# mLSTM projections: the gate panels' high parts made by GpSimd, and the low-rank blocks turned inside the gates' projection

## The reference, cut to what matters

```python
proj = h @ w_in                                    # [512, 1024] @ [1024, 1992]
u, v_m, o_pre, i_pre, f_pre, c_q, c_kv, k_r = split(proj)   # 512, 512, 512, 4, 4, 256, 128, 64 columns
u_c = silu(causal_dwconv(u, conv_w, conv_b))
q_m, k_m = u_h @ wq_m, u_h @ wk_m                  # per head
ig, fg = i_pre + b_igate, f_pre + b_fgate          # the recurrence's gates
hm = rmsnorm(mlstm_chunkwise(q_m, k_m, v_m, ig, fg))
y_m = sigmoid(o_pre) * hm                          # o_pre: the "gate panels" of the change
q_a = rmsnorm(c_q) @ w_uq                          # 256 -> 768, low rank
kv = rmsnorm(c_kv) @ w_ukv                         # 128 -> 1024, low rank
... per-head rmsnorm, rope, causal attention, rmsnorm -> y_a
out = concat([y_m, y_a]) @ w_out
```

## Time and profile before

| what | before |
|---|---|
| median of 3 runs | 1885.59 us (1885.58, 1885.59, 1886.93) |
| the profiled execution's own time | 1886.09 us |
| its span, first to last instruction | 1884.3 us |
| TensorE (PE) busy | 1847.6 us, 98% |
| GpSimd (POOL) busy | 1364.4 us, 72% |
| VectorE (DVE) busy | 907.7 us, 48% |
| ScalarE (ACT) busy | 756.6 us, 40% |

### The profile page before, as it was taken

One profiled execution on the slowest core, in us unless ns is written; L12 is line 12 of the kernel. 1 busy time (PEld: TensorE's weight loads), 2 busy tenths in 40 slices (PEclk: granted clock), 3 DMA queues, 4 the chain that ended last, 5 costly groups with the idle time before them and its releaser, 6 DMA issues.

```text
span 1884.3 us, 26203 instructions
## 1 busy us (share of the span) xinstructions
PE 1847.6 (98%) x9597; PEld 1560.9 (83%) x9597; DVE 907.7 (48%) x1797; ACT 756.6 (40%) x1459; POOL 1364.4 (72%) x1211
## 2 busy tenths in 40 slices
PE   7999999999999999999999999999999999999999
PEld 6888888888878887888888888987679888888887
DVE  6677777762028875355403412726753455203410
ACT  4577777754027763242102201567643522001100
POOL 8766666698854559879888988663524579888885
PEclk9999999999999999999999999999999999999999
DMA  7322222223432232422432333221122223332342
GB/s 223 110 68 68 68 68 67 68 68 90 111 105 75 63 95 90 136 68 89 112 89 90 104 96 89 70 82 45 46 68 90 90 67 90 94 107 90 89 110 69
DMA packets 213613, 165.71 MB, mean 88 GB/s; under 512 B 14478, under 2 KB 209873, under 8 KB 213122
## 3 DMA queue, kind: packets, MB, share of 16 engines
q1 hardware_dynamic: 208134, 149.32, 27.0%
q10 hardware_dynamic: 5372, 14.98, 2.4%
HBM read 161.11 MB, written 7.37 MB: 89 GB/s over the span
## 4 chain that ended last, share of the span: by engine, by line
PE 55%; POOL 5%; issue 2%; ACT 2%; DVE 2%; DMA 0%; POOLq 0%; ACTq 0%; DVEq 0%; SPq 0%
PE bank L401 42%; PE bank L483 4%; POOL w_lo L3254 3%; PE bank L427 1%; POOL w_hi L3246 1%; PE bank L1588 1%; PE bank L1612 1%; PE bank L3004 1%; PE bank L1810 1%; PE bank L1789 1%; PE bank L646 1%; PE bank L1799 0%; PE bank L2652 0%; PE bank L1598 0%; POOL x_features L750 0%
## 5 line engine op out<-in xcount | busy, mean ns | idle before, releaser
L3254 POOL TENSOR_TENSOR w_lo<-w_raw,w_hi 128x512 fp32r<-128x512 f32 (+1 forms) x572 | 718.0, 1288 | 207.6 <-ACT w_hi L1435 198.2
L3246 POOL TENSOR_TENSOR w_hi<-w_raw,one 128x512 fp32r<-128x512 f32 (+1 forms) x428 | 441.2, 1062 | 223.2 <-PE bank L401 199.6
L401 PE MATMUL bank<-h_hi,w_hi 128*128 128x512 f32 x952 | 377.4, 396 | 1.1 <-POOL w_lo L3254 0.8
L401 PE MATMUL bank<-h_hi,w_lo 128*128 128x512 f32 x952 | 371.9, 391 | 0.0
L401 PE MATMUL bank<-h_lo,w_hi 128*128 128x512 f32 x952 | 371.1, 390 | 0.0
L401 PE MATMUL bank<-a_hi,w_hi 128*128 128x512 f32 x832 | 326.0, 392 | 1.7 <-POOL w_lo L3254 1.4
L401 PE MATMUL bank<-a_hi,w_lo 128*128 128x512 f32 x832 | 324.0, 389 | 0.0
L401 PE MATMUL bank<-a_lo,w_hi 128*128 128x512 f32 x832 | 323.8, 389 | 0.0
L401 PEld LDWEIGHTS bank<-h_hi,w_lo 128*128 128x128 f32 x952 | 178.7, 188 | 39.0
L401 PEld LDWEIGHTS bank<-h_hi,w_hi 128*128 128x128 f32 x952 | 178.9, 188 | 35.5 <-issue 1.4
L401 PEld LDWEIGHTS bank<-h_lo,w_hi 128*128 128x128 f32 x952 | 179.1, 188 | 33.4
(11 more groups left out here) (506 smaller groups left out, 3021.6 us busy)
## 6 DMA issues: line engine op xcount, KB each, us to landing
w_raw<-in_w_ff SPq DMA_DIRECT2D x32, 1024.0 KB, 5.5
w_raw<-in_w_in SPq DMA_DIRECT2D x31, 1024.0 KB, 5.4
w_raw<-in_w_mlp_in SPq DMA_DIRECT2D x16, 1024.0 KB, 5.3
w_raw<-in_w_mlp_out SPq DMA_DIRECT2D x16, 1024.0 KB, 5.6
w_raw<-in_w_in SPq DMA_DIRECT2D x26, 512.0 KB, 4.2
w_raw<-in_w_ssd_out SPq DMA_DIRECT2D x8, 1024.0 KB, 5.6
bias_rows<-bias_row ACTq DMA_DIRECT2D x1, 4096.0 KB, 15.6
w_raw<-in_w_attn_out SPq DMA_DIRECT2D x4, 1024.0 KB, 5.8
```

What stands on the lines that cost most here:

```text
L401: mm = pe.matmul(bank[:, 0:ntok], a, b[:, koff + k, 0:ntok], start=(k == 0 and n == 0), stop=(k == L.kb - 1 and n == 2))
L3246: pool.tensor_tensor(w_hi[:, slot, part], raw[:, slot, part], one[:].broadcast_to([P, n]), ALU.mult).then_inc(split_hi, 1)
L3254: ins = pool.tensor_tensor(w_lo[:, slot, part], raw[:, slot, part], w_hi[:, slot, part].bitcast(F32), ALU.subtract)
```

## The change

Two edits. The gate panels leave `HIGH_BY_ACT`, and ScalarE's two calls of `split_high_act` for them go; GpSimd thereby makes their high parts with the instructions of line 3246, ahead of their low parts. And TensorE does the first two of L_if's 8 contraction steps, then the wait for `lt["low"]` and the 12 transposes of CQT and CKT, then L_if's other six steps; ScalarE's copy of the gates moves behind its three copies of the turned blocks.

```diff
-        HIGH_BY_ACT = ... + [L.p0 for L in (L_va, L_low, L_vb, *L_gate_m)] + ...
+        HIGH_BY_ACT = ... + [L.p0 for L in (L_va, L_low, L_vb)] + ...
...
             pe_panel_tokens(pe, L_vb, 0, 0, h_x)
-            pe_panel(pe, L_if, 0, 0, h_x)
+            pe_panel(pe, L_if, 0, 0, h_x, ks=range(0, 2))
             pe.wait_ge(lt["low"], 1)
             low = tp_n["pe"]
             pe_to_features(pe, CQT, T, 2, banks[4:6])
             pe_to_features(pe, CKT, T, 1, banks[6:7])
+            pe_panel(pe, L_if, 0, 0, h_x, ks=range(2, DB))
             pe.wait_ge(lt["kr"], 1)
...
             tokens_act(act, L_vb, 0, lambda t: VM[:, t, 3:5, 0:128], only=1)
-            gates_in_act(act)
             act_to_features(act, a_x, 8, 2, lambda b: colv("cq", b), T, banks[4:6])
             act_to_features(act, a_x, 10, 1, lambda b: colv("ckv"), T, banks[6:7])
+            gates_in_act(act)
             act.wait_ge(lt["kr"], 2)
             act.activation(KR, banks[7][:], ACT.Copy)
-            split_high_act(act, L_gate_m[0])
             for i in range(2 * T):
                 q_block_act(act, i)
...
             tokens_act(act, L_gate_m[0], 0, lambda t: OM[:, t, 0:256], ACT.Sigmoid)
-            split_high_act(act, L_gate_m[1])
             for i in range(2 * T):
                 k_block_act(act, i)
```

More of the change, by code:

```diff
@@ L1416, in ssd_stage_pe @@
             pe_panel(pe, L_ssd_out, 0, 0, a_x, ks=range(0, 2 * GROUPS - 2))
-        HIGH_BY_ACT = list(range(L_ssd[1][0].p0, L_gate_ssd.p0)) + [L_attn[1][0].p0, L_attn[1][1].p0] + [L_mlp[0][0][0].p0 + 1, L_u.p0 + 1] + [L.p0 for L in (L_va, L_low, L_vb, *L_gate_m)] + [L_out2.p0 + 2, L_out2.p0 + 3] + list(range(L_kx.p0, L_vx.p0 + 2))
+        HIGH_BY_ACT = list(range(L_ssd[1][0].p0, L_gate_ssd.p0)) + [L_attn[1][0].p0, L_attn[1][1].p0] + [L_mlp[0][0][0].p0 + 1, L_u.p0 + 1] + [L.p0 for L in (L_va, L_low, L_vb)] + [L_out2.p0 + 2, L_out2.p0 + 3] + list(range(L_kx.p0, L_vx.p0 + 2))
         high_by_act, low_by_dve = sem("high_by_act"), sem("low_by_dve")
```

## The result

The changed kernel takes 1889.08 us (median of 18 runs, 1887.4 to 1892.1), the kernel before 1885.79 us (median of 18 runs beside them, 1884.8 to 1887.4): a ratio of 1.0017 with a 95% interval of 1.0011 to 1.0024. That is 3.3 us slower, just inside 0.2%, outside my range, and to the side that I had given to rival (C) alone. The profiled execution took 1887.78 us, with a span of 1886.1.

The account below looks back on a forecast made before the run. TensorE, busy 98% of the span, bounds the kernel, with 5.5 us of waits between 1257 and 1300 us. Gains 0.8 (turn) and 1.8 (panels), less 0.6, 0.1 and 0.1, make 1.8 us: median 1883.8 us, range 1881.9 to 1886.4.

Parts of the forecast that it names:

- rival (C): Second gate panel late if GpSimd's two halves take over 12.1 us; slower, 1886.0 to 1886.8 us; chance 8%.
- Part 1: Turn of CQT and CKT moved inside the gates' projection: gain 0.8 us, at least 0.7, at most 0.95.
- (a): First gate panel's low part on GpSimd slows VectorE's softplus: cost 0.6 us taken, from nothing to 1.3.
- (b): VectorE's gate rows beside GpSimd's second gate panel: cost 0.1 us taken, ends -0.6 and +0.7.
- Rival B: The lock: softplus waits out the low part, first scan pays 0.7; gain only 0.6 us, 1884.6 to 1885.4; chance 18%.
- The first gate panel costs nothing: Panel ready on GpSimd at 1266.7, TensorE asks at 1269.3: cover 2.6 us, worst case 0.4 lost; work queued behind costs nothing.

Follow-up runs that it names:

- first_yield: Changed kernel with the second gate panel's high part back on ScalarE and GpSimd pausing for VectorE twice in the first panel's low part; ratio 0.9997.
- hold: Changed kernel, but GpSimd waits for VectorE's fourth query normalization before beginning the second gate panel; 1888.39 against 1886.11 us, ratio 1.0010.
- fill: Changed kernel with 14 extra matmuls of 128x512 ahead of the fourth turn, in TensorE's wait before the fifth; 1888.18 us, ratio 1.0003.
- turn_only: Changed kernel with both gate panels' high parts back on ScalarE, leaving only the turn inside the gates' projection; 1886.70 against 1886.93 us, ratio 1.0000.
- high_only: Changed kernel with the gates' projection in one piece again, both gate panels' high parts still on GpSimd; 1888.36 against 1886.93 us, ratio 1.0007.
- fill_turns: Changed kernel with 28 extra transposes ahead of the fourth turn as filler for TensorE's wait; one execution, 1890.52 us.
- first_panel: Changed kernel with the second gate panel's high part back on ScalarE, only the first's on GpSimd; 1888.57 us, ratio 1.0009.
- small_pieces: Changed kernel, but GpSimd splits the second gate panel in 16 pieces of 128x128 per part instead of 4 of 128x512; 1889.76 us, ratio 1.0016.
- half_yield: hold_yield, but ScalarE makes half of the second gate panel's high part and GpSimd the other half; 1885.52 against 1887.22 us, ratio 0.9991.
- hold_yield: Changed kernel with the pauses of first_yield and GpSimd's wait of hold, both gate panels on GpSimd; 1888.05 against 1887.22 us, ratio 1.0005.
- second_panel: Changed kernel with the first gate panel's high part back on ScalarE, only the second's on GpSimd; 1887.00 us, ratio 1.0001.

## Why the prediction was wrong

**Part 1 was right in its place.** I took 0.8 us for the turn. L_uq starts 1.04 us earlier in every kernel that has it, and the gate columns, not the low parts, are what is late next. Without the overlaps in its way, 0.7 us of it reach the fifth turn (first_yield).

**The step that failed: what GpSimd's second panel costs VectorE.** I listed the fourth normalization beside that panel only as something that slows GpSimd (rival C), and priced the overlap with VectorE in two other places, (a) the softplus and (b) the gate rows. Its six operations had the same two-tile form as L2321, whose row showed 0.84 against 0.42 us. They took 7.65 us instead of 2.5, each 0.6 to 1.1 us longer than before, at most a piece. I also took ScalarE's 24 copies to be ScalarE's own time (1.8 us earlier, so 1.8 us gained) and left out that from the fifth block on each square waits for a sum that stands behind the normalization on VectorE: 3.3 us of wait took the place of the 1.8 us copy. hold removes the overlap, and the fifth turn moves from 43.78 to 40.34.

**The second omission: the wait is paid twice.** I had no rival in which a longer wait of TensorE lowers its clock. The fill run holds the clock at 1.00 with everything before it unchanged and gets back 1.8 us. For the sum: I had TensorE reach the second gate panel 2.0 us early. Measured, the fifth turn comes 1.4 us late, and 1.8 us more go to the clock behind it: 3.2 us of loss.

**Term (a) had its bound wrong, and its price about right.** In the changed kernel the softplus took 1.5 us more (3.17 against 1.71), above the upper end of 1.3 us: it overlapped GpSimd's low part for 1.8 us, where I had 1.5. And in turn_only, high_only and fill_turns L2373 alone took 1.28, 2.86 and 3.91 us. I had started the overlap at the softplus; L2373 and L2375 come before it, in the middle of the low part, and L2373 can be held until the part ends. What reached the chain when it was not held was smaller than the stretch: first_panel and first_yield differ by 0.5 us at the fifth turn, against the 0.6 that I took.

**Term (b) came out at the lower end of its bounds, and not for its reasons.** I took a loss of 0.1 us, with ends of -0.6 and +0.7. The gate rows took from 1292.94 to 1299.41 us, 6.5 us, against 7.1 before. The first scan did not meet the low part (1.21 us in both), and the last operation was 1.15 us in both; L2387 between the scans took 0.68 us instead of 1.35.

**Rival C came true in its sign and not in its mechanism.** GpSimd needed 4.85 + 5.43 = 10.3 us, below the 12.1 from which I had it decide, and TensorE never waited for that panel. Rival B (VectorE late in ScalarE's place) had the right mechanism, but at other operations, and at a price that left a gain of 0.6 us; the measured price was more than the gain. "The first gate panel costs nothing" held for the panel (TensorE did not wait for it), not for VectorE.

**The rule that the prediction cites**, of the Trainium skill, "SBUF — State Buffer", section "Who interferes with whom", was the one to believe. By it each of the normalization's six operations, which have two inputs in SBUF, could lose a piece; with 1.28 us for a piece (10.3 us for eight) that is an estimate of up to 7.7 us, and the trace has 5.2. I read it against the softplus alone. It states that the loser is blocked for the whole instruction; L2373 and the scan of small_pieces show more than that, a loser blocked through several instructions in a row. And of the softplus the changed kernel held L971 and L972 (0.60 and 1.21 us instead of 0.17), which have one tile as input; the rule as I cited it, for two inputs, does not name them.

What stays open: when VectorE gets its turn between two pieces and when it does not. In the profiles without the pauses L2373 took 0.77 us in the kernel before, 0.19 to 0.21 us in six others and 1.28 to 3.91 us in four. fill and fill_turns fall on both sides with the same start within 0.01 us, so the kernel does not settle it, and no run here shows what does. How much of the measured 3.3 us comes in other executions from L2373 and how much from the second panel is open for the same reason: the split above is that of the profiled ones. The run-to-run spread of all kernels comes at least in part from falls of the clock elsewhere (near 808, 1170 and 1430 us), which I did not try to take away.

## What to carry to other kernels

Moving a piece of work to an idle engine must be priced on every engine that shares something with it: go along the other engine's timeline through the whole new interval, and take each operation of the contended form at its contended price. Then look for what stands behind those operations in their queue, for here the sums, not the normalization, were what ScalarE needed. A wait that grows from 1.2 to 3 us on the bound engine is to be counted with the clock that it may cost. And half the work moved can be worth more than all of it: the stage of half_yield ends 2.3 us before that of hold_yield, which moves the whole panel with the same waits.

## What the runs showed of the hardware

- A VectorE operation with two tiles in SBUF can wait for GpSimd's current piece: 128x256 (L2321) took 0.42 us alone, 0.84 beside pieces of L_ukv's split, 1.38 beside those of 128x512, 0.51 beside those of 128x128. Reductions (L2498, 0.42 us) were not touched.
- It can also be held through several pieces: 16 columns for 3.91 us (fill_turns), a scan of 4x512 for 8.82 us (small_pieces), both until GpSimd's row of instructions ended. The operation on 16 columns, started at the same place, took 0.21 us in fill.
- It goes the other way too: a GpSimd piece of 128x512 took 2.20 us instead of 1.28 beside VectorE's scan (hold).
- Sixteen pieces of 128x128 took 7.08 us where four of 128x512 took 4.85, both beside VectorE.
- TensorE's granted clock fell to 0.50 in or behind waits of 1.95 us (turn_only), 2.4 us (hold, hold_yield), 2.8 us (second_panel), 3.0 us (small_pieces), 3.4 us (high_only), 4.5 us (fill_turns) and 1.25 + 3.15 us (changed). It stayed at 1.00 behind the 1.2 us of the kernel before, behind 1.66 us (first_panel) and behind another wait of 1.95 us (second_panel). The fall of the changed kernel cost 1.8 us by the fill run, and 14 matmuls in the wait prevented it.
